# A hybrid SSM and attention block followed by a banded attention block: the prelude's modulation sums shared between two engines, one feed-forward's end regrouped by token pairs, and three waits cut into pieces

## The reference

```python
# first block
mod = silu(c) @ w_ada + b_ada                    # 6 x 1024 numbers: sh1, sc1, g1, sh2, sc2, g2
h = x * (1 + sc1) + sh1
y = hybrid_mixer(h)                              # h @ w_in, SSD scan + forgetting attention, @ w_out
x = layer_norm(ALPHA * x + (1 + g1) * y)
h = x * (1 + sc2) + sh2
ff = square(relu(h @ w_ff_in)) @ w_ff_out
x = layer_norm(ALPHA * x + (1 + g2) * ff)
# second block
h = rms_norm(x); p = h @ w_in_2                  # q, k, v, conv and pooling inputs
x = x + concat(band_attention, short_conv, pooling) @ w_out_2
x = x + square(relu(rms_norm(x) @ w_mlp1_2)) @ w_mlp2_2
```

## Time and profile before

| | us |
|---|---|
| median of 3 runs (lowest, highest) | 1378.03 (1376.95, 1379.72) |
| the profiled execution, its own time | 1377.24 |
| its span, first to last instruction | 1375.5 |
| PE matmuls busy | 1324.8 (96% of the span) |
| DVE busy | 836.8 (61%) |
| ACT busy | 657.6 (48%) |
| POOL busy | 623.4 (45%) |
| mean granted TensorE clock | 0.995 |

### The profile page before, as it was taken

How to read it: one execution, slowest core, us unless ns; L and a number is a source line. 1 busy time by engine, 2 the same in 40 slices (tenths; PEclk the granted TensorE clock), 3 DMA queues, 4 the chain that set the end, 5 groups by cost and what they waited for, 6 DMA issues and landing times.

```text
span 1375.5 us, 16594 instructions
## 1 busy us (share of the span) xinstructions
PE 1324.8 (96%) x6471; PEld 1090.6 (79%) x6471; DVE 836.8 (61%) x1151; ACT 657.6 (48%) x919; POOL 623.4 (45%) x503
## 2 busy tenths in 40 slices
PE   2999999999999999999999996999999999999999
PEld 2888778888878888888888875887788888888887
DVE  6586987789861677708158396648722661906337
ACT  0645445466774165445353455424535544545353
POOL 0453855433335856251443505673744535153440
PEclk9999999999999999999999998999999999999999
DMA  9343534755324525867769543225133686766953
GB/s 341 114 109 124 118 123 147 207 157 172 116 64 154 165 82 127 219 161 151 229 126 254 129 104 122 92 92 128 52 99 124 142 225 150 165 203 153 244 122 92
DMA packets 149837, 202.93 MB, mean 148 GB/s; under 512 B 10140, under 2 KB 94384, under 8 KB 148480
## 3 DMA queue, kind: packets, MB, share of 16 engines
q1 hardware_dynamic: 123760, 146.95, 34.0%
q0 software_dynamic: 19760, 49.53, 17.7%
q10 hardware_dynamic: 6240, 5.40, 1.6%
HBM read 189.12 MB, written 2.26 MB: 139 GB/s over the span
## 4 chain that ended last, share of the span: by engine, by line
PE 87%; DVE 7%; POOL 2%; ACT 1%; issue 1%; DMA 1%; SPq 0%; ACTq 0%; DVEq 0%; POOLq 0%
PE bank L2098 26%; PE bank L2100 26%; PE bank L2099 26%; DVE tmp L1642 2%; PE bank L2304 2%; POOL w_lo L686 2%; PE bank L2314 1%; DMA arena<-in_w_ada_dram 1%; PE bank L2725 1%; PE bank L2497 1%; PE bank L2289 1%; PE bank L2317 1%; PE bank L2279 1%; PE bank L2498 1%; POOL w_lo L824 1%
## 5 line engine op out<-in xcount | busy, mean ns | idle before, releaser
L686 POOL TENSOR_TENSOR w_lo<-raw,w_hi 128x512 fp32r<-128x512 f32 x180 | 260.2, 1475 | 274.4 <-ACT w_hi L937 274.4
L2098 PE MATMUL bank<-w_hi,a_hi 128*128 128x512 f32 x864 | 341.3, 395 | 9.4 <-DVE a_lo L1433 6.2
L2100 PE MATMUL bank<-w_hi,a_lo 128*128 128x512 f32 x864 | 337.9, 391 | 0.0
L2099 PE MATMUL bank<-w_lo,a_hi 128*128 128x512 f32 x864 | 337.7, 391 | 0.0
L2098 PE MATMUL bank<-a_hi,w_hi 128*128 128x512 f32 (+1 forms) x832 | 321.4, 386 | 2.7 <-DVE a_lo L1433 1.7
L2100 PE MATMUL bank<-a_hi,w_lo 128*128 128x512 f32 (+1 forms) x832 | 317.5, 382 | 0.0
L2099 PE MATMUL bank<-a_lo,w_hi 128*128 128x512 f32 (+1 forms) x832 | 317.5, 382 | 0.0
L824 POOL TENSOR_TENSOR w_lo<-raw,w_hi 128x512 fp32r<-128x512 f32 x112 | 150.9, 1452 | 180.4 <-ACT w_hi L1060 180.4
L2098 PEld LDWEIGHTS bank<-w_hi,a_hi 128*128 128x128 f32 x864 | 163.1, 189 | 47.1 <-issue 10.2
L2100 PEld LDWEIGHTS bank<-w_hi,a_lo 128*128 128x128 f32 x864 | 162.9, 189 | 34.3
L2099 PEld LDWEIGHTS bank<-w_lo,a_hi 128*128 128x128 f32 x864 | 163.2, 189 | 32.6
(11 more groups left out here) (279 smaller groups left out, 1696.1 us busy)
## 6 DMA issues: line engine op xcount, KB each, us to landing
raw<-in_w_in_dram SPq DMA_DIRECT2D x24, 1024.0 KB, 5.2
raw<-in_w_mlp_dram SPq DMA_DIRECT2D x24, 1024.0 KB, 6.0
arena<-in_w_ada_dram SPq DMA_DIRECT2D x18, 1024.0 KB, 6.6
raw<-in_w_ff_in_dram SPq DMA_DIRECT2D x16, 1024.0 KB, 7.7
arena<-in_w_ff_out_dram POOLq DMA_DIRECT2D x13, 1024.0 KB, 8.7
arena<-in_w_mlp_dram POOLq DMA_DIRECT2D x13, 1024.0 KB, 8.6
raw<-in_w_out_dram SPq DMA_DIRECT2D x12, 1024.0 KB, 5.5
raw<-in_w_in_dram SPq DMA_DIRECT2D x16, 512.0 KB, 5.4
```

Of the source, the lines that this page charges most:

```text
L686: last = pool.tensor_tensor(w_lo[:, u0 % 2, cols], raw[:, u0 % 2, cols], w_hi[:, u0 % 2, cols].bitcast(F32), ALU.subtract)
L2098: pe.matmul(out_, hi_a, hi_b, start=start, stop=False, skip_group_check=resumed)
L2099: pe.matmul(out_, hi_a, lo_b, start=False, stop=False, skip_group_check=resumed)
L2100: return pe.matmul(out_, lo_a, hi_b, start=False, stop=stop, skip_group_check=resumed)
```

## The change

Five groups of edits.

1. **Prelude, sums.** For n = 1 to 3 DVE weighs 6 of the 8 blocks (`WEIGHED`); PE multiplies the last two blocks directly, 8 fp32 matmuls with one moving column, and `sum_columns` adds to the same columns. The fourth part comes as two DMAs.
2. **Prelude, order.** The dt and forget columns are loaded before x, x and the first XBC unit as two halves each. PE transposes k 0 to 3, then k 4 to 7 in the first steps of the loop. ACT writes the first subtracted part right behind the first `a_hi`; DVE makes `a_lo` of k = 0 before the XBC unit's high part, which it writes as two halves between the `a_lo`. POOL makes `dt_lo` only after the fourth weighing.
3. **Three waits.** `z_half(2, 0)` waits quarter by quarter for its unit, the scores of chunk 3 come as two instructions of 8 heads, and the second unit of `U_WO2` is waited for by quarters.
4. **End of the first feed-forward.** In the last quarter DVE gates, adds and gathers statistics in 2-token blocks. The block of M2 is finished earlier; M3's block is finished at once, M4's products are gated, the shifts follow, and M7's and M4's blocks are added behind the first items. ACT copies high parts A_S3 and A_S4 earlier (in every quarter). The items go pair by pair. SP may load `U_QKV2` one unit earlier.
5. **QKV units.** POOL makes both roots of token blocks 2 and 3 within unit +1, units +2, +3, +4 are waited for by quarters, `rms_root` moves behind unit +4, `head_root(0, 0)` behind +5. ACT makes the high parts of +2 and +3 after all items and before the squares.

```diff
             def prelude():
...
-                for n in range(1, 4):
+                for n in range(1, 3):
                     sp.dma_start(ada[:, n], w_ada_v[:, :, n * 512:n * 512 + 512]).then_inc(ada_in[n], 16)
-                sp.dma_start(xtok, x_v).then_inc(x_in, 16)
-                columns(0, 0, U_XBC, w_in_v, C_XBC + P * XBC_ORDER[0])
+                for half in range(2):
+                    rows_ = slice(4 * half, 4 * half + 4)
+                    sp.dma_start(ada[:, 3, rows_], w_ada_v[:, rows_, 1536:2048]).then_inc(ada_last[half], 16)
...
+                for half in range(2):
+                    cols = slice(512 * half, 512 * half + 512)
+                    sp.dma_start(xtok[:, :, cols], x_v[:, :, cols]).then_inc(x_in[half], 16)
...
+            def direct_columns(n):
+                pe.wait_ge(ada_in[n] if n < 3 else ada_last[1], 16)
+                for k in range(WEIGHED, KT):
+                    for h in range(4):
+                        col = 256 + 4 * n + h
+                        pe.matmul(bank[7][:, col:col + 1], ada[:, n, k, P * h:P * h + P], cact[:, k:k + 1], start=k == WEIGHED and h == 0, stop=False, skip_group_check=True)
+
             for n in range(4):
+                if n:
+                    direct_columns(n)
                 pe.wait_ge(ada_sum, n + 1)
-                sum_columns(tmp[:, n % 2], 7, 256 + 4 * n, 4, col_mm)
-            pe.wait_ge(x_in, 16)
-            turn(xtok, KT - 1)
-            pe.wait_ge(mod_made, 1)
-            turn(xtok, 1, KT - 1)
+                sum_columns(tmp[:, n % 2], 7, 256 + 4 * n, 4, col_mm, resumed=n > 0)
+            pe.wait_ge(x_in[0], 16)
+            turn(xtok, 4)
...
+                for k in range(KT):
+                    if k == 1:
+                        dve.wait_ge(xbc_half, 16)
+                        dve.tensor_copy(w_hi[:, U_XBC % 2, 0:1024], raw[:, U_XBC % 2, 0:1024]).then_inc(w_hi_made, 1)
+                    elif k == 3:
...
+                    split_affine(M_H, k, mod[:, 8 + k:9 + k])
...
-                    dve.tensor_tensor(b4, b4, c4, ALU.mult).then_inc(score_made, 1)
+                    if ch < TB - 1:
+                        dve.tensor_tensor(b4, b4, c4, ALU.mult).then_inc(score_made, 1)
+                    else:
+                        for g in range(2):
+                            dve.tensor_tensor(b4[:, g], b4[:, g], c4[:, g], ALU.mult).then_inc(score_made, 1)
...
+            def finish(step):
+
+                if step == 0:
+                    add_copied(READ_M2, OP_M2, 2)
+                    gate(READ_M2)
+                elif step == 1:
+                    add_block(READ_M2, 9)
+                else:
+                    add_copied(READ_M3, OP_M3, 4)
+                    gate(READ_M3)
+                    add_block(READ_M3, 10)
+                    read_product(U_FF1 + FF_OPS * (QUARTERS - 1), QUARTERS - 1, READ_M4, OP_M4, gate_product)
+                    shift(1, 0)
+                    shift(1, 1)
+                    gate(READ_M7)
+                    split_item(0, M_N2, lambda k: mod[:, 64 + k:65 + k])
+                    split_item(1, M_N2, lambda k: mod[:, 64 + k:65 + k])
+                    add_block(READ_M7, 11)
+                    split_item(2, M_N2, lambda k: mod[:, 64 + k:65 + k])
+                    split_item(3, M_N2, lambda k: mod[:, 64 + k:65 + k])
+                    dve.wait_ge(c_read, reads(QUARTERS - 1, READ_M4))
+                    add_block(READ_M4, 12)
...
                 ff_hi(u0, g, OP_M6)
+                split_high(sq[:, 0:4, 256:512], 0)
                 ff_hi(u0, g, OP_M5)
+                act.wait_ge(s_made, 4 * g + S_S4)
+                split_high(sq[:, 4:8, 0:256], 1)
                 if last:
                     copy_product(READ_M6, OP_M6, -1.0)
-                split_high(sq[:, 0:4, 256:512], 0)
-                act.wait_ge(s_made, 4 * g + S_S4)
-                split_high(sq[:, 4:8, 0:256], 1)
...
             feed_forward(U_FF1, 0, ff_v[0][1])
-            lo(U_QKV2, turn=1, root_at=1)
-            for t in range(2, TB):
-                ln_root(1, t)
+            lo(U_QKV2, turn=1)
+            both_parts(U_QKV2 + 1, (2, 3))
...
-            lo(U_QKV2 + 2)
+            lo(U_QKV2 + 2, parts=lo_part)
             relative_mask()
-            lo(U_QKV2 + 3)
+            lo(U_QKV2 + 3, parts=qkv_part)
+            lo(U_QKV2 + 4, parts=qkv_part)
             rms_root(2, EPS2)
-            lo(U_QKV2 + 4)
+            lo(U_QKV2 + 5)
             head_root(0, 0)
-            lo(U_QKV2 + 5)
             head_root(0, 1)
             lo(U_CP)
```

More of the change, by code:

```diff
@@ L112 @@
 HALVES_Q = 6
-LN_ITEMS = [(pair, 4 * half + k) for half in range(2) for pair in range(2) for k in range(4)]
+LN_ITEMS = [[(pair, 4 * half + k) for half in range(2) for pair in range(2) for k in range(4)], [(pair, k) for pair in range(2) for k in range(8)]]
 XS_BANKS = (4, 5)
@@ L595, in _ @@
             feed_forward(U_FF1, 0, *ff_v[0], [(sum_made, 1)])
-            four_rows(U_QKV2, w_in2_v, 0, 0)
+            for b in range(2):
+                sp.wait_ge(w_lo_made, U_QKV2 + b - 2)
+                rows(0, 0, U_QKV2 + b, w_in2_v, 4 * b, 0, split=False)
+            for b in range(2, 4):
+                rows(0, 0, U_QKV2 + b, w_in2_v, 4 * (b % 2), 512)
             for b in range(2):
@@ L665, in both_parts @@
                 for part in range(4):
+                    if part == 2:
+                        for t in roots:
+                            ln_root(1, t)
                     cols = slice(512 * part, 512 * part + 512)
@@ L802, in _ @@
             lo(U_WO2)
-            lo(U_WO2 + 1)
+            lo(U_WO2 + 1, parts=wo_lo)
             rms_root(1, RMS_EPS)
@@ L945, in turned_hi, with normalize @@
                     act.activation(a_hi[buf][:, k], bank[b][:], ACT.Identity, scale=scale, bias=bias).then_inc(a_hi_made, 1)
-            def normalize(turn, t):
+            def normalize(turn, t, halves=range(2)):
                 act.wait_ge(ln_shift, 2 * turn + t + 1)
-                for part in (slice(0, 512), slice(512, 1024)):
+                for half in halves:
+                    part = slice(512 * half, 512 * half + 512)
                     act.activation(x1[:, t, part], x1[:, t, part], ACT.Identity, scale=st[:, 8 + t:9 + t], bias=st2[:, 4 + t:5 + t]).then_inc(xhat_made, 1)
@@ L979, in affine_items @@
                         act.wait_ge(a_lo_made, t0 + j - 1)
[L980 removed]
+                    act.activation(a_hi[0][:, k, tokens(pair)], turned_item(turn, pair, k), ACT.Identity, scale=scale(k), bias=bias(k)).then_inc(a_hi_made, 1)
                     rest(j)
@@ L1618, in feed_forward @@
[L1618 to L1628 removed]
+                    split_low(g, A22, sq[:, 4:8, 256:512], 2)
@@ new lines, in feed_forward @@
+                    product_lo(u0, g, OP_M4)
+                    last(2)
+                else:
+                    product_lo(u0, g, OP_M5)
+                    read_product(u, g, READ_M6, OP_M6, add)
+                    split_low(g, A_S3, sq[:, 0:4, 256:512], 0)
+                    product_lo(u0, g, OP_M7)
+                    read_product(u, g, READ_M5, OP_M5, add)
+                    split_low(g, A_S4, sq[:, 4:8, 0:256], 1)
+                    product_lo(u0, g, OP_M3)
+                    read_product(u, g, READ_M7, OP_M7, add, READ_M5)
+                    split_low(g, A22, sq[:, 4:8, 256:512], 2)
+                    product_lo(u0, g, OP_M4)
@@ L1636, in weigh @@
                 link(dve.tensor_scalar(acc, src(0), cact[:, 0:1], None, ALU.mult))
-                for k in range(1, KT):
+                for k in range(1, blocks):
                     if k == KT // 2 and middle:
@@ L1972, in residual @@
                     dve.scalar_tensor_tensor(x1[:, t], x1[:, t], ALPHA, yacc[:, t], ALU.mult, ALU.add).then_inc(z_made, 1)
-            def gate_and_add(t, half, count, made):
-                part = slice(512 * half, 512 * half + 512)
-                if count is not None:
-                    dve.wait_ge(c_read, count)
-                    link(dve.tensor_tensor(yacc[:, t, part], yacc[:, t, part], row[:, 3, part], ALU.mult))
-                dve.tensor_tensor(x1[:, t, part], x1[:, t, part], yacc[:, t, part], ALU.add).then_inc(sum_made, 1)
-                dve.wait_ge(sum_made, made)
-                half_stats(t, half, 1 - t // 2)
@@ L1995, in last_product, with block_of, gate @@
-            def last_product(n, t, part, product, negative):
-                dve.tensor_tensor(yacc[:, t, part], product[:], row[:, 3, part], ALU.mult).then_inc(c_read, 1)
-                dve.wait_ge(c_read, reads(QUARTERS - 1, READ_M4, t - 2))
-                gate_and_add(t, 0, None, 13 + t)
+            def block_of(n):
+                pair, half = c_block(n)
+                return slice(2 * pair, 2 * pair + 2), slice(512 * half, 512 * half + 512)
+            def gate(n):
+                ts, part = block_of(n)
+                dve.wait_ge(c_read, reads(QUARTERS - 1, n))
```

(19 more changed lines are left out.)

208 lines of the change are left out of this document (105 added, 103 removed).

## The result

The changed kernel takes **1380.45 us** (median of 12 runs, 1378.99 to 1382.98); the kernel before, run beside it, 1377.86 (12 runs). The ratio is 1.0018, 95% interval 1.0011 to 1.0025: 0.2% slower, where 9.6 us of gain were forecast. The profiled execution took 1380.96, its span is 1379.2 (before 1375.5), its mean clock 0.993.

A forecast was written before the change was run, and what follows sets the result against it. PE, 96% busy, was taken as the bound, so only its waits and low-clock work could be won: 2.5 + 1.0 + 0.8 + 0.8 + 5.7 - 1.2 = 9.6 us, giving 1368.3 us, range 1366.9 to 1370.5 (chance 0.52).

The forecast's parts named there:

- part 5: QKV units behind the first feed-forward: `rms_root` behind unit +4 ends POOL's chain about 2 us later, a loss of 1.2 us.
- The prelude: Start of the kernel: six weighed blocks, direct columns and the new load order win 2.5 us, bounds 1.5 and 4.3.
- z: PE's 0.97 us wait for a whole z unit goes when it waits by quarters: 1.0 us won.
- Scores: DVE's 3.26 us score instruction becomes two, so PE's whole 0.82 us wait goes: 0.8 us won.
- `U_WO2`: PE's wait for the second unit of these weights goes when it waits by quarters: 0.8 us won.
- The feed-forward's end: Turn to the second block: PE reaches `row_pair` of +2 (time T) 5.7 us earlier, bounds 7.0 and 2.7.
- The shared port: DVE's gates beside POOL's units lock each other out; four meetings at 1.3 us would leave 1.8 us of gain.
- Given back to POOL: Rival: behind T POOL binds units and roots, loss 3 to 5 us instead of 1.2: 1371 to 1372.5; chance 0.13.
- The slower case: Rival: the clock halves before the first item and stays low for all 16 items, total near 1389; chance 0.04.
- No change: Rival: gains and losses cancel within 0.2% (2.8 us), total 1378; chance 0.04.
- signs of being wrong: PE waiting over 1 us for x or half unit, over 5 at item 4, over 2 for line 987's reads or roots.
- one of being right: Sign in the profile: PE waits under 1.5 us in all from the fifth item to the band attention.

The follow-up runs named there:

- root_only: The changed kernel with POOL's two roots in the order from before the change, the load of `U_WO3` not held back: 1370.46 us.
- hold_wout: The changed kernel with SP's first load of `U_WO3` held back until the four band copies have landed: 1373.44 us.
- hold_root: hold_wout with POOL's old order, `rms_root` ahead of unit +4 and `head_root(0, 0)` ahead of unit +5: 1369.95 us.
- hold_z: hold_wout with the piecewise z wait given also to the second unit of the pair, `z_half(2, 1)`: 1373.52 us.
- ffend_root: The kernel before with groups 4 and 5 of the change, but POOL's roots in their old order: 1373.92 us.

## Why the prediction was wrong, point by point

- **The step that failed is part 5.** It put `rms_root` behind unit +4, saw that POOL's chain "ends about 2 us later against T than today, where POOL stood still", let it end at k's normalization, and took 1.2 us, bounds 0 and 3. The chain doesn't end there: k's normalization releases ACT's four band copies, and these run against SP's load, which is released by POOL's unit and not by the root. The 2 us were too few as well. Against T the last root of k starts at 51.6 us (909.39) where it started at 45.5 (911.75), 6.1 later: POOL's 5.5 us behind the root, for a high part that ACT makes only behind the reads, weren't counted. Between copies and load 2.3 us were lost (7.0 to 4.7). It costs 10.0 us in the changed kernel (root_only), 9.8 in the kernel before: 7.0 for the collision and its clock (hold_wout) and 3.5 for PE's waits on late reads and roots (hold_root), the half us between being within the bounds. No bound of mine held this; with the early root the kernel takes 1370.5, at the edge of my forecast: that is 7.5 us below before, where my terms without part 5 sum to 10.8.
- **The prelude** was right in its parts (2.2 for 2.5) and wrong in that all of it reaches the end: 0.4 measured alone. A fetch of instructions makes the last copy land 1 us later. Before, shows no wait there, but the slack was 0.2 us: the last copy, issued at 932.35, landed 8.2 us later, at 940.6, and PE began the step at 940.8.
- **z**: 0 for 1.0. The wait was read at the wrong unit. The sequence of 24 matmuls ahead of it shows which `z_half` waits. hold_z shows that the right place would have brought nothing either, since DVE's chain is next: "nothing within 20 us" was wrong, it came 5 us later.
- **Scores**: the wait of 0.8 went, and 0.6 of it stood again at 199, by the same chain; that the cut makes DVE's work itself longer (4.40 for 3.26) wasn't counted. **`U_WO2`**: 0.9 for 0.8.
- **The feed-forward's end**: from 500 to T the lead grew by 7.2, forecast 5.7, just above the bounds of 7.0 and 2.7. The two waits for `product_lo` are gone. Only one of the gates was held up (2.37 for 1.22) instead of the 1.3 us for several, and the clock was back to full for item 4. The mechanism was right, the size a little low.
- **The shared port**: the rule that I weighed for the gates (the Trainium skill, "SBUF — State Buffer", "Who interferes with whom") speaks of just the pair that met: a VectorE operation with two SBUF inputs and a GpSimd one that reads. It bit at one gate only (2.37), and above all behind T, where I had looked at order only: 1.22 against 2.3 us for DVE, 5.0 against 8.9 for POOL's unit, at most 2.6 us in the end.
- **Rivals.** "Given back to POOL" (3 to 5 us, 0.13) names the right engine and place; the small waits behind T came to 4.4 as it says. The slower case was the wrong one: the clock didn't stay low for 16 items, it read 0.79 in 832 to 837 us and 1.00 from there on. That the kernel is slower came from a transfer, and no rival held a transfer. "No change" (0.04) has the nearest number, 2.6 us from none, but by no cause that it names. None of my signs of being wrong showed (0.6 us at the first XBC quarter, 0.7 at item 4, 0.6 for ACT's reads), while one of being right, under 1.5 us of waits from item 4 to the band attention, failed with 3.5. No sign watched the place where it went wrong.

**Open.** In the changed kernel's profile the clock is 0.5 from 489 to 496 us and the lead falls from 3.4 to 1.35; in the earlier trace rows's execution it isn't. root_only and hold_root show it too, hold_wout for half as long, ffend_root and hold_z not. What sets it off wasn't tested. It also blurs small differences: root_only's five executions are three of 1370.0 to 1370.5 and two of 1372.4 and 1372.8, the profiled one among the latter.

## What to carry to other kernels

Follow a delayed step to its last consumer on every engine, the DMA queues too, and ask which transfer starts at the same moment from another chain: here one POOL instruction, made 2 us later, put 2 MB and 1 MB side by side and cost ten us, seven by the meeting and three by late reads. Write down the slack of transfers that show no wait; it is the margin of every later change. And where an elementwise pass is moved, look at what GpSimd does in the same microseconds.

The best kernel here is the changed one with the old order of the two roots: 1370.46, 0.5% below before; with the load held as well 1369.95.

## What the runs showed of the hardware

- An instruction fetch of one 16 KB packet among 2 MB of copies delays their landing by 0.4 to 1.2 us (medians of 7.1 and 7.2 against 7.6 to 8.3; the last copy 8.2 to 8.4 against 9.2 to 9.5), so 24 added matmuls in the prelude change a wait 900 us later.
- 200 waits that are already met cost PE about 10 us, 50 ns each (12.85 against 2.67 for its first transposes); 90 cost 4.3.
- A DVE operation with two SBUF inputs and a POOL subtraction side by side take 1.8 to 1.9 times as long as alone (2.32 for 1.22, 8.88 for 5.03), so side by side they do hardly more than one after the other.
